# Attention stage: natural tiles for the local head group, head groups merged as they come, attention units beside two of three or every second projection step

## What is computed

```python
q = (xn @ w_q).reshape(bsz, seq, 3, 8, 64)
for gi, (window, dilation) in enumerate(((128, 1), (512, 4), (2048, 16))):
    o, lse = dilated_window_group(q[:, :, gi], k_sh[:, :, gi], v_sh[:, :, gi], window, dilation)
alpha = softmax(stack(lses), axis=0)            # over the three groups
o = sum(alpha[..., None] * stack(outs), axis=0)
return o.reshape(bsz, seq, 512) @ w_o
```

## Time and profile before

| | us |
|---|---|
| median of three runs (lowest, highest) | 1728.95 (1724.18, 1729.76) |
| profiled execution, its own time | 1725.64 |
| its span, first to last instruction | 1723.9 |
| TensorE matmul busy | 1470.3 (85%) |
| VectorE busy | 1022.7 (59%) |
| ScalarE busy | 827.3 (48%) |
| GpSimd busy | 355.9 (21%) |

### The profile page before, as it was taken

How to read it: one execution, slowest core, us unless ns; L and a number is a source line. 1 busy time by engine, 2 the same in 40 slices (tenths; PEclk the granted TensorE clock), 3 DMA queues, 4 the chain that set the end, 5 groups by cost and what they waited for, 6 DMA issues and landing times. The chain is left out here.

```text
span 1723.9 us, 29826 instructions
## 1 busy us (share of the span) xinstructions
PE 1470.3 (85%) x11787; PEld 1116.2 (65%) x11787; DVE 1022.7 (59%) x1261; ACT 827.3 (48%) x1201; POOL 355.9 (21%) x323
## 2 busy tenths in 40 slices
PE   4899995677779889999982899999984899999980
PEld 2283881666775477887772677777774677777870
DVE  5333338445654478989873424444445489989873
ACT  3223224344430258888862333334442358888851
POOL 1000007645551013232313000000001012232302
PEclk8698996698989989999995999999975899999995
DMA  4042205013142489999964321111200589999954
GB/s 154 1 146 98 73 25 209 14 31 87 53 128 71 154 276 382 378 381 380 382 241 153 98 89 49 50 49 50 73 1 0 188 277 386 385 383 375 383 212 153
DMA packets 172089, 302.47 MB, mean 175 GB/s; under 512 B 34480, under 2 KB 44848, under 8 KB 171984
## 3 DMA queue, kind: packets, MB, share of 16 engines
q1 hardware_dynamic: 159408, 271.59, 44.0%
q0 software_dynamic: 11520, 25.19, 4.0%
q10 hardware_dynamic: 1056, 4.19, 0.6%
HBM read 279.96 MB, written 35.65 MB: 183 GB/s over the span
## 5 line engine op out<-in xcount | busy, mean ns | idle before, releaser
L1376 DVE TENSOR_TENSOR moe_wlo<-moe_raw,moe_whi 128x2048 fp32r<-128x2048 f32 x160 | 365.6, 2288 | 38.9 <-ACT moe_whi L1372 34.6
L1372 ACT ACTIVATE moe_whi<-moe_raw 128x2048 fp32r<-128x2048 f32 x192 | 366.9, 1916 | 23.6 <-PE all_bank L1385 22.3
L1383 PE MATMUL all_bank<-moe_whi,moe_xhi 128*128 128x512 f32 x512 | 208.2, 407 | 4.1 <-DVE moe_xlo L1432 4.1
L1384 PE MATMUL all_bank<-moe_wlo,moe_xhi 128*128 128x512 f32 x512 | 200.8, 392 | 0.0
L1385 PE MATMUL all_bank<-moe_whi,moe_xlo 128*128 128x512 f32 x512 | 200.7, 392 | 0.0
L1383 PEld LDWEIGHTS all_bank<-moe_whi,moe_xhi 128*128 128x128 f32 x512 | 96.6, 189 | 27.5 <-DVE moe_xlo L1432 4.4
L1385 PEld LDWEIGHTS all_bank<-moe_whi,moe_xlo 128*128 128x128 f32 x512 | 96.8, 189 | 21.3
L1384 PEld LDWEIGHTS all_bank<-moe_wlo,moe_xhi 128*128 128x128 f32 x512 | 96.9, 189 | 18.3
L1383 PE MATMUL all_bank<-moe_whi,moe_hhi 128*128 128x512 f32 x256 | 102.3, 399 | 7.6 <-DVE moe_hlo L1456 7.6
L1384 PE MATMUL all_bank<-moe_wlo,moe_hhi 128*128 128x512 f32 x256 | 101.6, 397 | 0.0
L1385 PE MATMUL all_bank<-moe_whi,moe_hlo 128*128 128x512 f32 x256 | 101.3, 396 | 0.0
(11 more groups left out here) (410 smaller groups left out, 3142.2 us busy)
## 6 DMA issues: line engine op xcount, KB each, us to landing
moe_raw<-in_moe_w_gate_dram SPq DMA_DIRECT2D x64, 1024.0 KB, 9.5
moe_raw<-in_moe_w_up_dram SPq DMA_DIRECT2D x64, 1024.0 KB, 9.6
moe_raw<-in_moe_w_down_dram SPq DMA_DIRECT2D x64, 1024.0 KB, 8.5
attn_xhat<-in_w_kv_dram SPq DMA_DIRECT2D x10, 1024.0 KB, 5.2
out_dram<-all_gain SPq DMA_DIRECT2D x1, 8192.0 KB, 22.3
attn_xhat<-in_attn_w_q_dram SPq DMA_DIRECT2D x6, 1024.0 KB, 5.0
all_h<-in_rwkv_w_v_dram SPq DMA_DIRECT2D x4, 1024.0 KB, 8.5
all_h<-in_rwkv_w_k_dram SPq DMA_DIRECT2D x4, 1024.0 KB, 6.7
```

The source lines that it names most:

```text
L1372: nc.scalar.activation(whi[slot % SPLITS][:, :], raw[slot % 6][:, :], ACT.Copy).then_inc(m["hi_ok"], 1)
L1376: nc.vector.tensor_tensor(wlo[slot % SPLITS][:, :], raw[slot % 6][:, :], whi[slot % SPLITS][:, :].bitcast(fp32), ALU.subtract).then_inc(m[ ...
L1383: nc.tensor.matmul(bank[b][:, :], hi[:, k0 + k, :], wh[:, k, :], start=begin and k == 0, stop=False)
L1384: nc.tensor.matmul(bank[b][:, :], hi[:, k0 + k, :], wl[:, k, :], start=False, stop=False)
```

## The change

- **Group 0 in natural tiles.** The copies out of PSUM put k, q and v of group 0 in the order of time: for k and q by a rearranged access pattern, for v by four copies of 32 partitions each instead of one of 128. The query tile j then needs only the key tiles j-1 and j. A unit is now a head and a *pair* of query tiles (`jp`), each against 256 keys: 16 units in the place of 32, with 128x512 scores as before. The values take three or four matmuls. VectorE's copy out of PSUM becomes eight copies of 32 partitions x 64, which bring the output back in the order of residues. GpSimd moves the maxima and sums of group 0 in the same way with 16 small copies.
- **Scores two units at a time.** `scores(u)` runs for even u and makes the scores of two heads. Its matmuls alternate between the lower and the upper 64 partitions and between two banks.
- **Running merge.** Groups 1 and 2 take the minimum of their own negated maximum and of the one so far. GpSimd works out the difference, ScalarE its exponential (the *fade*), GpSimd the new row sums and, for group 1, the faded output; VectorE then adds the unit's output from PSUM. For group 2 the last reciprocal (VectorE) and the scaling by it (GpSimd) come in the loop too. The combination after the units is gone.
- **Placement.** Group 0 takes two of three steps (24 steps of slices 3 to 5), group 1 every second (16 steps of slices 6 and 7), group 2 every step of slice 8. The value products of group 2 come after the loop, for two heads at a time in a bank of their own (`far_values`), with a multiplication and an addition of 128x512 on VectorE for each pair (`far_output`).
- **The end.** The transposes (`turn`), the splits and the output products are interleaved with these, pair by pair. The last block of `w_o` is split behind them.

The core of the diff:

```diff
-        units = [(0, hh, (j,)) for hh in range(AH) for j in range(J)] + [(gi, hh, tuple(range(J))) for gi in (1, 2) for hh in range(AH)]
+        units = [(0, hh, jp) for jp in range(J // 2) for hh in range(AH)] + [(gi, hh, None) for gi in (1, 2) for hh in range(AH)]
+        MID, FAR_AT = 2 * AH, 3 * AH
...
         def beside(sl, kh, i):
-            u = 8 * (sl - BESIDE) + 4 * kh + i
-            return u if 0 <= u < AH * (J + 1) else None
+            q = 8 * (sl - BESIDE) + 4 * kh + i
+            if 0 <= q < 24:
+                return 2 * (q // 3) + q % 3 if q % 3 < 2 else None
+            if 24 <= q < 40:
+                return (q - 24) // 2 + MID if q % 2 else None
+            return q - 40 + FAR_AT if q >= 40 else None
...
+        def copies(u):
+            if u // 12:
+                return [(projected(u), bank_of(u)[:, :])]
+            if u % 12 // 4 < 2:
+                return [(projected(u).rearrange("p (j r i) -> p r j i", r=J, j=J), bank_of(u)[:, :].rearrange("p (r j i) -> p r j i", r=J, j=J))]
+            r = u % 4
+            return [(vv[0][32 * r:32 * r + 32, j, :], bank_of(u)[32 * j:32 * j + 32, :]) for j in range(J)]
...
         # GpSimd
+            for r in range(J):
+                for j in range(J):
+                    ins = nc.gpsimd.tensor_copy(stat[32 * j:32 * j + 32, r, :, :], near[32 * r:32 * r + 32, j, :, :])
+                    ins.then_inc(stat_ok, 1)
+            for u in range(MID, NU):
+                fading(u)
+                row_sums(u)
+                if u < FAR_AT:
+                    near_faded(u)
+                elif u > FAR_AT:
+                    scale(u - 1)
+            scale(NU - 1)
...
         # ScalarE
+                if gi > 0:
+                    act.wait_ge(d_ok, u - MID + 1)
+                    nc.scalar.activation(fold(fade[gi], hh), fold(fade[gi], hh), ACT.Exp).then_inc(e_ok, 1)
...
         # VectorE
+                if gi == 0:
+                    for i in range(2):
+                        j = 2 * jp + i
+                        for r in range(J):
+                            ins = V.tensor_copy(oacc[32 * j:32 * j + 32, r, HD * hh:HD * hh + HD], bank[7][32 * r:32 * r + 32, HD * i:HD * i + HD])
+                else:
+                    dve.wait_ge(faded, hh + 1)
+                    ins = V.tensor_tensor(sums(hh), bank[7][:, 0:HD * J].rearrange("p (j v) -> p j v", j=J), sums(hh), ALU.add)
...
+            far_output(0)
+            far_output(1)
+            rest(0)
+            far_output(2)
+            rest(1)
+            far_output(3)
+            rest(2)
+            rest(3)
+            split_lo(dve, NP + 1)
...
         # TensorE
             def scores(u):
-                if u >= 2:
-                    pe.wait_ge(sm_ok, u - 1)
-                b = bank[4 + u % 2]
-                for i, j in enumerate(js):
-                    q = qT[gi][rows, hh // 2, P * j:P * j + P]
-                    out, k = (b[:, :], kT[gi][rows, hh // 2, :]) if gi == 0 else (b[:, P * i:P * i + P], kT[gi][rows, hh // 2, P * j:P * j + P])
-                    ins = nc.tensor.matmul(out, q, k, start=True, stop=True)
+                if u >= 2:
+                    pe.wait_ge(sm_ok, u)
+                for i in range(2 if gi == 0 else J):
+                    for e in range(2):
+                        rows = slice(HD * e, HD * e + HD)
+                        j, n = (2 * jp + i, 2 * P) if gi == 0 else (i, P)
+                        k0 = P * max(j - 1, 0) if gi == 0 else P * j
+                        ins = nc.tensor.matmul(bank[4 + e][:, n * i:n * i + n], qT[gi][rows, hh // 2, P * j:P * j + P], kT[gi][rows, hh // 2, k0:k0 + n], start=True, stop=True)
...
             def attend(u):
-                scores(u)
-                if u >= 2:
+                if u % 2 == 0:
+                    scores(u)
+                if 2 <= u < FAR_AT + 2:
                     values(u - 2)
                 if u >= 1:
                     transposes(u - 1)
...
+            transposes(NU - 1)
+            far_values(0)
+            far_values(1)
+            turn(0)
+            far_values(2)
+            turn(1)
+            far_values(3)
+            turn(2)
+            pe.wait_ge(lo_ok, NP + 1)
+            for u in range(3):
+                pe.wait_ge(merged, u + 1)
+                product(u, range(0, 2))
+            turn(3)
+            for u in range(3):
+                product(u, range(2, 3))
+            product(3, range(0, 3))
+            for u in range(4):
+                product(u, range(3, 4))
             pe.wait_ge(lo_ok, NP + 2)
+            for u in range(J, 2 * J):
+                product(u, range(4))
```

More of the change, by code:

```diff
@@ L2153, in _ @@
                             dve.wait_ge(unit, u + 1)
[L2154 to L2167, removed]
-            dve.wait_ge(p_ok, NU)
[L2170 to L2179, removed]
@@ L2245, in values @@
                     pe.wait_ge(o_ev, u)
[L2246 to L2250 removed]
+                else:
+                    pe.wait_ge(m2_ok, 1)
+                v = lambda tile: vv[gi][:, tile, HD * hh:HD * hh + HD]
@@ new lines, in values @@
+                if gi == 0:
+                    for i in range(2):
+                        j = 2 * jp + i
+                        for x in range(2 if j else 1):
+                            at = 2 * P * i + P * x
+                            ins = nc.tensor.matmul(bank[7][:, HD * i:HD * i + HD], pT[u % 2][:, at:at + P], v(max(j - 1, 0) + x), start=x == 0, stop=x == 1 or j == 0)
+                else:
+                    for j in range(J):
+                        ins = nc.tensor.matmul(bank[7][:, HD * j:HD * j + HD], pT[u % 2][:, P * j:P * j + P], v(j), start=True, stop=True)
@@ new lines, in values, with far_values @@
+                ins.then_inc(o_done, 1)
+            def far_values(hp):
+                if hp == 0:
+                    pe.wait_ge(o_ev, FAR_AT)
+                    evacuated(pe, NPROJ - 2)
+                    evacuated(pe, NPROJ - 1)
+                elif hp < 3:
+                    pe.wait_ge(sm_ok, NU)
+                pe.wait_ge(pt_ok, FAR_AT + 2 * hp + 2)
+                for e in range(2):
+                    for j in range(J):
+                        hh, at = 2 * hp + e, J * HD * e + HD * j
+                        ins = nc.tensor.matmul(far_bank(hp)[:, at:at + HD], kept[hh][:, P * j:P * j + P], vv[2][:, j, HD * hh:HD * hh + HD], start=True, stop=True)
+                ins.then_inc(far_done, 1)
@@ new lines, in turn, with product @@
+            def turn(b):
+                pe.wait_ge(merged, b + 1)
+                for j in range(J):
+                    ins = nc.tensor.transpose(bank[b][:, P * j:P * j + P], oacc[:, j, P * b:P * b + P], g["ident"][:, :])
+                ins.then_inc(otr, 1)
+            def product(u, kts):
+                half, j = u // J, u % J
+                for kt in kts:
+                    pe.wait_ge(ol_ok, kt + 1)
+                    ins = three_passes(out_bank(u)[:, :], [v[:, kt, P * j:P * j + P] for v in (oh, ol)], [v[half][:, kt, :] for v in (whi, wlo)], kt == 0, kt == W // P - 1)
+                if W // P - 1 in kts:
+                    ins.then_inc(out_done, 1)
```

228 lines of the change are left out of this document (126 added, 102 removed).

## The result

| | before | after |
|---|---|---|
| median of four runs (lowest, highest), us | 1729.35 (1724.18, 1729.76) | 1651.37 (1647.60, 1652.53) |
| profiled execution, us | 1725.64 | 1652.53 |

The account below looks back on a forecast made before the run. TensorE bounds the projections, chains of waits the rest. Saved: 53.1 (slices 3 to 7) - 2.3 (seams) - 0.5 (GpSimd) + 32.9 (slice 8 and end) = 83.2; 1725.64 less that is 1642.4, given as 1643; own range 1634 to 1652, 8-in-10 1628 to 1669.

Parts of the forecast that it names:

- A pair of scores: Scores of two units on TensorE, alternating halves and banks: 1.2 us a pair, bounds 1.05 and 2.10.
- my sum for it: TensorE's work in slices 3 to 7: projections 111.6, group 0 21.4, group 1 11.6, scores 14.4; 159.0 us.
- The stops: Waits in slices 3 to 7: 2.3 us for seams, v copies and mask, 0.5 for GpSimd slowing VectorE.
- it just fits: Unit behind a weight split, slices 3 to 7: VectorE's eight copies end at 16.3, values need them at 16.4.
- 0.21 foreseen: VectorE's eight 32 x 64 output copies per group 0 unit: 0.21 us each, 1.7 a unit, bounds 1.0 and 3.2.
- The slow rival: Copies between quadrants make it slower than before; gain gone at 1.1 us a copy, 1754 at 1.3; chance 0.03.
- my 0.5 us for it: GpSimd's work slowing VectorE's splits and minima in slices 6 to 8: 0.5 us on the path, bounds 0 and 8.
- the walk: Chain from slice 8's start: TensorE loses 3.7 and 4.6 us behind splits, last projection ends at 40.2, products at 76.2.
- I add 6: Low clock for far values, turns and products at the end: 6 us on 76.2, making 82.2; bounds 0 and 14.
- Two halves that don't run side by side: Rival: score pairs in slices 3 to 7 and slice 8 cost 0.9 us more each, 14.4, so 1657; chance 0.23.
- VectorE and ScalarE don't set the pace: Rival that they do: ten splits each stop TensorE 1.5 us in slices 3 to 7, 2 for slice 8, 1660; chance 0.16.
- 33 us as one thing: Slice 8 and the end: 115.1 us before against 82.2 after, 32.9 saved.

Follow-up runs that it names:

- E6: Changed kernel without the copies that move data between groups of 32 partitions (group 0's token order then wrong): 1643.63 us.
- E4: Changed kernel plus 28 matmuls whose results nobody reads, filling TensorE's waits around the last pair's scores and before the last transposes: 1638.59 us.
- E5: Changed kernel with both heads of a score pair reading the lower 64 rows, so on one half of the array: 1661.62 us.
- E7: Kernel before plus natural tiles for group 0 and the new placement of groups 0 and 1; scores unpaired, group 2 behind the loop, old combination: 1689.78 us.
- E3: Changed kernel with the value products of group 2's first two pairs before the last transposes, the first pair merged before the last reciprocal: 1641.76 us.
- E1: Changed kernel with a pair's score matmuls in two runs of one half each instead of alternating halves: 1651.16 us.
- E8: Changed kernel with E3's order, E4's 14 fills around the last pair's scores, group 0 at second and third of three steps: 1635.47 us.

## Why the prediction was right, and where it was off

**The time and the gain.** The measured median is 8.4 us above the 1643. Of these, 5.2 are gain that did not come (83.2 against 78.0). The other 3.1 are the start of the sum: it takes the gain from the profiled execution (1725.64), which was 3.7 below the median of four, and adds back only 0.6.

**Slices 3 to 7: 161.8 foreseen, 162.4 measured.** Two errors cancel, and that is luck. A pair of scores was priced at 1.2 and is 1.07; steps and seams were a little cheaper too, and the values of the last two units fell into slice 8. Without any stop the window is 154.4 (E6) and my sum for it was 159.0. The stops were priced at 2.8 and are 7.9 (E6). I had put three copies of 0.69 in front of the first unit; the trace has eight, 5.6 us in a row, for both of VectorE's projections of v. And I let "it just fits" stand for a chain whose slack I had at 0.1 us.

**The copies: 0.21 foreseen, 0.22 measured each, 1.87 for eight in a row.** They don't overlap, as the rule on quadrants in the Trainium skill ("VectorE: DVE Perf Modes", "Two Vector instructions with no wait between them") has it; the trace agrees, with 0.23 from start to start against the 0.13 of three unmoved ones. E6 has the better comparison, two copies out of the same bank that change no quadrant, 0.35 us for both, so 0.13 from start to start:

```profile
1044.09 0.35 DVE L2193 COPY attn_oacc<-all_bank 128x64 f32<-128x64 f32 x2
```

The slow rival needed 1.1 us and has nothing left.

**GpSimd.** The 16 moves of maxima take 3.9 us from the first to the end of the last, 0.19 each, and no wait on them shows. A split beside GpSimd's work takes 0.747 for an instruction, as before: no slowing shows, and my 0.5 us for it had no place.

**Slice 8: end of the last projection foreseen 40.2 us after the slice's start, measured 41.9 (its last matmul starts at 41.6).** Both stops stand where the walk put them: idle 1.26 and 1.44, then 2.46 and 1.44, 6.6 in all where I had 8.3. The 1.7 saved go into a low clock from 1226, for which I had nothing here: it makes the last step 4.8 and not 2.6, and E4 measures it at 2.5. The last 0.9 us of the difference are not traced.

**The end: the step that was mis-sized.** The term is "I add 6" for the clock, with bounds 0 and 14. E4 measures it at 11.7, 2.5 of them in slice 8 and 9.2 behind it: with the clock full, slice 8 and the end take 74.9, and my sum without the clock was 76.2. At half the clock the far values were 3.4 us for a pair and not 1.9, and they were on the path in full, not "half": until 1253 TensorE works in a row and VectorE waits for it. Of the 5 us between the forecast gain of 83.2 and the 78.0 measured, this term is 5.7, and the rest nearly balances.

**A small one.** The walk has 1.7 us from turn 0 (48.9) to the split's end (50.6), without a row for its two parts; ScalarE's copy and VectorE's remainder take 1.09 and 1.07, as their rows of the kernel before would have told (3.76 and 3.92 for four). It had no effect, since the far values were later.

**The rivals.** Two halves that don't run side by side are out: they do (E5), and the rule on tiles in parallel in the Trainium skill ("TensorEngine Tiling (Array Packing)", "Key Properties") agrees, with 1.07 against 1.92 us. VectorE and ScalarE don't set the pace in general, but stop TensorE at two places (E6). The gain by part: I credited slice 8 with 33 us as one thing. Slice 8 and the end gave 28.3. The ablations give 27.1 to the merging and the end and 3.8 to the placement beside slice 8, less the 2.6 by which E7 was longer there than the kernel before. The prediction had no such parts.

## What to carry to other kernels

Price a wait of TensorE by what follows it as well as by itself. Here 3.5 us of waiting cost some 9 more in the work behind it (E4), and bringing independent work of TensorE into the wait (E3) was worth three times the wait, nearly all of it by the clock. When a chain is walked and "just fits", give it the price of not fitting, with the clock. And before moving units under other work, work out the chain they run through when alone: beside slice 8 the eight units were only 3.8 us cheaper than behind it in the traces, and 1.5 by the medians.

## What the runs showed of the hardware

- Two sets of 64-row matmuls on different halves and banks take 1.07 us where one half takes 1.92, also when the sets stand behind each other by four instructions; with eight shorter ones each, 1.64 (E1, E5).
- Copies on VectorE that change the group of 32 partitions each time start 0.23 us apart, and two that change none 0.13 apart (after, E6).
- TensorE's granted clock fell to 0.50 (1.2 GHz) behind idle stretches of 1.8 and 2.2 us as well as behind those of 3.5 to 4.6. It stayed up behind 1.26 and 1.44 us at 1205 in the changed kernel, and where the waits were filled with matmuls that nobody reads (E4). The same stops had both outcomes: the 1.8 us late in group 0 left it up in E1, the 1.26 and 1.44 us lowered it in E6, and 1.83 us in front of the products lowered it in E8 and not in E3. So one execution doesn't tell whether a short stop costs its low clock.
